# Spreading the five links of an expert pair over five positions, with u rows and v rows gathered apart

## What is computed

```python
def _peer(u, wq, keys, pu, pv):
    ...
    def block(args):
        xb, ib, gb = args
        act = jax.nn.gelu(jnp.einsum('thkd,td->thk', jnp.take(pu, ib, axis=0), xb), approximate=False) * gb
        return jnp.einsum('thk,thkd->td', act, jnp.take(pv, ib, axis=0))
```

## Time and profile before

| | us |
|---|---|
| median of 3 runs | 4927.02 (4921.54 to 4928.32) |
| the profiled execution | 4904.76 |
| its span, first instruction to last | 4903.0 |
| PE busy | 3672.0 (75%) |
| DVE busy | 3083.1 (63%) |
| POOL busy | 1563.8 (32%) |
| the gathers' packets, share of 16 DMA engines | 68.7% |

### The profile page before, as it was taken

How to read it: one execution, slowest core, us unless ns; L and a number is a source line. 1 busy time by engine, 2 the same in 40 slices (tenths; PEclk the granted TensorE clock), 3 DMA queues, 4 the chain that set the end, 5 groups by cost and what they waited for, 6 DMA issues and landing times.

```text
span 4903.0 us, 39211 instructions
## 1 busy us (share of the span) xinstructions
PE 3672.0 (75%) x11564; PEld 1854.1 (38%) x11564; DVE 3083.1 (63%) x7016; ACT 1117.4 (23%) x2809; POOL 1563.8 (32%) x1416
## 2 busy tenths in 40 slices
PE   8872987755887877976776589785488787797776
PEld 3430465531432432433443237563133343242222
DVE  1236537768686686684356654775867668668555
ACT  0101224411212212222421123441121221221111
POOL 0101223313344344343222312321333434444443
PEclk9985998867999999998988789887799999999999
DMA  8564785577999999999877868656699999999998
GB/s 295 180 239 178 281 293 215 207 272 290 404 384 421 379 402 420 375 394 368 327 287 299 349 231 322 219 202 258 260 406 383 411 398 391 421 373 415 391 421 357
DMA packets 314581, 1607.83 MB, mean 328 GB/s; under 512 B 41632, under 2 KB 82848, under 8 KB 144384
## 3 DMA queue, kind: packets, MB, share of 16 engines
q0 software_dynamic: 184320, 1342.26, 68.7%
q1 hardware_dynamic: 129952, 262.99, 14.8%
q10 hardware_dynamic: 96, 0.10, 0.0%
HBM read 1568.02 MB, written 37.20 MB: 327 GB/s over the span
## 4 chain that ended last, share of the span: by engine, by line
PE 37%; DMA 24%; DVE 21%; issue 7%; ACT 4%; SPq 4%; POOL 2%; POOLq 1%; DVEq 0%; ACTq 0%
DMA big<-in_experts,big 19%; PE bank L1979 15%; DVE big L1374 7%; PE bank L1729 4%; PE bank L1724 4%; PE bank L1955 3%; PE bank L1678 2%; POOL big L2088 2%; PE bank L1926 2%; DMA big<-in_w_in 1%; ACT big L1629 1%; DVE big L1282 1%; DVE big L1284 1%; DMA big<-in_iota 1%; SPq L862 1%
## 5 line engine op out<-in xcount | busy, mean ns | idle before, releaser
L1979 PE MATMUL bank<-big 128*128 128x512 f32 x4608 | 2333.6, 654 | 939.8 <-ACT big L1629 938.9
L2088 POOL DMA_INDIRECT big<-in_experts,big x1280 | 1452.2, 1135 | 3043.1 <-PE bank L1979 2593.1
L1374 DVE CUSTOM_DVE_ANT_0 big<-big 128x1024 f32<-128x1024 f32 x1280 | 1548.2, 1228 | 570.7 <-DMA big<-in_experts,big 569.9
L1979 PEld LDWEIGHTS bank<-big 128*128 128x128 f32 x4608 | 907.7, 206 | 2254.2 <-ACT big L1629 1267.8
L1629 ACT ACTIVATE big<-big 128x128 f32<-128x128 f32 x1152 | 407.8, 396 | 1201.7 <-DVE big L1352 1191.6
L1639 ACT ACTIVATE big<-big 128x2 f32<-128x2 f32 x640 | 130.9, 204 | 1600.8 <-DVE big L1374 1600.3
L1352 DVE TENSOR_TENSOR big<-big 128x2 f32<-128x2 f32 x640 | 108.5, 170 | 256.9 <-ACT big L1639 201.9
L1729 PE MATMUL bank<-big 128*128 128x256 f32 x960 | 220.7, 387 | 19.4 <-DMA big<-in_w_in 18.1
L1724 PE MATMUL bank<-big 128*128 128x128 f32 (+1 forms) x768 | 214.8, 435 | 2.0 <-DMA big<-in_w_in 2.0
L1729 PEld LDWEIGHTS bank<-big 128*128 128x128 f32 x960 | 185.0, 194 | 60.5 <-DMA big<-in_w_in 21.8
L1678 PE MATMUL bank<-big 128*2 128x512 f32 x384 | 172.5, 603 | 18.4 <-DMA big<-in_b_ada 11.0
(11 more groups left out here) (243 smaller groups left out, 2880.7 us busy)
## 6 DMA issues: line engine op xcount, KB each, us to landing
big<-in_w_ada SPq DMA_DIRECT2D x24, 2048.0 KB
big<-in_w_in SPq DMA_DIRECT2D x48, 1024.0 KB, 8.2
big<-in_experts,big POOLq DMA_INDIRECT x1280, 10.2
big<-modd SPq DMA_DIRECT2D x34, 512.0 KB, 21.8
big<-in_w_out SPq DMA_DIRECT2D x4, 4096.0 KB, 20.3
big<-in_peer_wq SPq DMA_DIRECT2D x4, 4096.0 KB, 39.1
y_d<-big SPq DMA_DIRECT2D x20, 512.0 KB, 5.6
big<-y_d SPq DMA_DIRECT2D x20, 512.0 KB, 11.0
```

Source lines behind the costliest of these rows:

```text
L1374: v_.tensor_tensor_reduce(ring[:, j, 0:D], ring[:, j, 0:D], EU[it % 2], 1.0, 0.0, ALU.mult, ALU.add, DOT[:, n % 16:n % 16 + 1]).then_inc(e ...
L1979: i = mm(ps[4 + h][:, :], DG[:, q % DIAGS * P:(q % DIAGS + 1) * P], ring[:, n % RING, D + 512 * h:D + 512 * h + 512], start=first, stop=last)
L2088: g_.indirect_dma_start(ring[:, n % RING, :], None, io["experts"], bass.IndirectOffsetOnAxis(ap=IDX[it % 2].bitcast(U32)[:, n:n + 1], axis ...
```

## The change

`apart(it)` is true for tiles 0, 4 and 5. In them the links of pair G stand at five positions: the dots at G, the GELU at G+1, `weigh` at G+2, `diag` at G+3, `v_pair` and DVE's own sums at G+4. In the other tiles all stays at G and G+1, but never ahead of an earlier pair, so the first pairs behind a heavy tile wait for its last ones. A v half is now needed four positions after its u half, and the ring still has eight slots. So in the heavy tiles, and for the first four pairs of the tile behind one (`halved`), u and v rows come by two gathers of 4 KB rows from two new inputs, `peer_u` and `peer_v` (the same numbers as `experts`). The u gather waits for the dot eight slots earlier (`e_dot`), the v gather stands one position behind its pair's dots and waits for the sum eight slots earlier. Consumers of v wait for a semaphore of their own (`e_gatv`). The tail of a heavy tile stands three positions later, and g0 of the tiles behind them goes from 7 to 10.

```diff
@@ order_of_work
-            (1, TICK["mx", 1, "smd"] + 1, TICK["mx", 2, "smd"], 7, 58),
+            (1, TICK["mx", 1, "smd"] + 1, TICK["mx", 2, "smd"], 10, 58),
...
+def apart(it):
+    return it in (0, 4, 5)
+
+def tail_place(it):
+    return 4 if apart(it) else 1
+
+def stands_at(near, far):
+    table, at = {}, 0
+    for G in range(DEPTH * TILES * PAIRS):
+        at = max(at, G + (far if apart(G // PAIRS) else near))
+        table.setdefault(at, []).append(G)
+    return table
+
+GELU_AT, WEIGH_AT, DIAG_AT, VALUE_AT = stands_at(0, 1), stands_at(1, 2), stands_at(1, 3), stands_at(1, 4)
+
+def halved(N):
+    G = N // 2
+    return apart(G // PAIRS) or (G >= 4 and apart((G - 4) // PAIRS))
+
+def value_loads(N):
+    return 16 * sum(1 for n in range(N % RING, N + 1, RING) if halved(n))
...
@@ DVE
+                        if halved(N):
+                            ve.wait_ge(e_gatv[n % RING], value_loads(N))
...
-                if G and (it < ALL or g == 0):
-                    weigh(G - 1)
+                for G in WEIGH_AT.get(at, ()):
+                    weigh(G)
+                for G in VALUE_AT.get(at, ()):
+                    value_sums(G)
...
-                if it and 2 <= g < 6:
-                    tail(it - 1, g - 1)
+                if it and 1 <= part < 5:
+                    tail(it - 1, part)
@@ ACT
-                if it < ALL or g == 0:
-                    diag(G - 1)
...
+                for G in DIAG_AT.get(it * PAIRS + g, ()):
+                    diag(G)
+                for G in GELU_AT.get(it * PAIRS + g, ()):
+                    gelu(G)
@@ PE
+                    if halved(N):
+                        pe.wait_ge(e_gatv[n % RING], value_loads(N))
...
-                if G and (it < ALL or g == 0):
-                    v_pair(G - 1)
+                for G in VALUE_AT.get(it * PAIRS + g, ()):
+                    v_pair(G)
@@ POOL
+                if halved(N):
+                    if N >= RING:
+                        ge.wait_ge(e_dot, N - RING + 1)
+                        ge.sem_inc(passed, 1)
+                    g_.indirect_dma_start(ring[:, n % RING, 0:D], None, io["peer_u"], offset(N)).then_inc(e_gat[n % RING], 16)
+                else:
+                    slot_done(N)
+                    g_.indirect_dma_start(ring[:, n % RING, :], None, io["experts"], offset(N)).then_inc(e_gat[n % RING], 16)
+
+            def gather_value(N):
+                j = N % RING
+                if N >= RING:
+                    slot_done(N)
+                g_.indirect_dma_start(ring[:, j, D:2 * D], None, io["peer_v"], offset(N)).then_inc(e_gatv[j], 16)
 
             def expert(it, g):
-                goal = min(2 * (it * PAIRS + g) + RING, ALL * SLOTS)
+                at = it * PAIRS + g
+                for N in (2 * at - 2, 2 * at - 1):
+                    if N >= 0 and halved(N):
+                        gather_value(N)
+                goal = min(2 * at + RING, ALL * SLOTS)
                 while len(issued) < goal and scored(len(issued) // SLOTS):
                     gather(len(issued))
```

More of the change, by code:

```diff
@@ L438, in build @@
         e_gat = [sem(f"e_gat{j}") for j in range(RING)]
+        e_gatv = [sem(f"e_gatv{j}") for j in range(RING)]
         e_vd = sem("e_vd")
@@ L882, in expert @@
             def expert(it, g):
-                if g == 3 and it in (1, 5, 6):
+                if it in (1, 5, 6) and g == tail_place(it - 1) + 2:
                     sp.wait_ge(e_tail.sem, e_tail.at(it - 1, "r02" if shared(it - 1) else "r01"))
@@ L886, in expert @@
                     load_g2(it)
-                if g == 6 and it:
+                if it and g == tail_place(it - 1) + 5:
                     sp.wait_ge(e_tail.sem, e_tail.at(it - 1, "xb"))
@@ L1352, in weigh, with value_sums @@
                 v_.tensor_tensor(AW[:, c], AG[:, c], GW[it % 2][:, 2 * g:2 * g + 2], ALU.mult).then_inc(e_aw, 1)
+            def value_sums(G):
+                it = G // PAIRS
                 for N in (2 * G, 2 * G + 1):
@@ L1364, in expert @@
             def expert(it, g):
-                G = it * PAIRS + g
-                if g == 1 and it:
+                at = it * PAIRS + g
+                part = g - tail_place(it - 1)
+                if it and part == 0:
                     tail(it - 1, 0)
-                if G and (it < ALL or g == 0):
-                    weigh(G - 1)
+                for G in WEIGH_AT.get(at, ()):
+                    weigh(G)
+                for G in VALUE_AT.get(at, ()):
+                    value_sums(G)
                 if it < ALL:
@@ L1630, in diag, with gelu @@
                                   scale=AW[:, N % 16:N % 16 + 1]).then_inc(e_dg, 1)
+            def gelu(G):
+                c = slice(2 * G % 16, 2 * G % 16 + 2)
+                ae.wait_ge(e_dot, 2 * G + 2)
+                a_.activation(AG[:, c], DOT[:, c], ACT.Gelu).then_inc(e_ge, 1)
             def expert(it, g):
-                G = it * PAIRS + g
-                if it < ALL or g == 0:
-                    diag(G - 1)
[L1636 to L1640, removed]
+                for G in DIAG_AT.get(it * PAIRS + g, ()):
+                    diag(G)
+                for G in GELU_AT.get(it * PAIRS + g, ()):
+                    gelu(G)
+                if it and g == tail_place(it - 1) + 3:
                     ae.wait_ge(e_tail.sem, e_tail.at(it - 1, "mv"))
@@ L2071, in _, with slot_done, offset @@
             issued, passed_tick = [], [-1]
+            def slot_done(N):
+                if summed_by_vector(N - RING):
+                    ge.wait_ge(e_vd, by_vector(N - RING))
+                else:
+                    ge.wait_ge(e_v, by_tensor(N - RING))
+                ge.sem_inc(passed, 1)
+            def offset(N):
+                it, n = divmod(N, SLOTS)
+                return bass.IndirectOffsetOnAxis(ap=IDX[it % 2].bitcast(U32)[:, n:n + 1], axis=0)
             def gather(N):
                 it, n = divmod(N, SLOTS)
[L2075 to L2081, removed]
+                if N == 0:
                     for u in range(3):
@@ L2096, in expert @@
                     issued.append(1)
-                assert it == ALL or len(issued) >= 2 * (it * PAIRS + g) + 2
+                assert it == ALL or len(issued) >= 2 * at + 2
             def scored(it):
```

15 lines of the change are left out of this document (7 added, 8 removed).

## The result

The changed kernel took 4868.92 us in the median of four runs (4866.19 to 4874.52), the kernel before 4924.28 beside it (4912.35 to 4928.32): a ratio of 0.9893, interval 0.9873 to 0.9913, 55 us less. The prediction said 4864, 63 us less.

A forecast was written before the change was run, and what follows sets the result against it. Light tiles were taken as DMA-bound, heavy tiles as engines waiting for each other. Terms -38 - 56 - 13 - 18 - 17 + 7 + 64 + 8 = -63 us took the 4927.0 median to 4864, range 4785 to 4930.

The forecast's parts named there:

- Rival (a): Scans of heavy tiles: all waits go, so they run at the busier engine, 71 us more gained, 4793; chance 0.15.
- (b): Hand-overs to light tiles cost their upper bound, 60 us more: 4924, no change; chance 0.14.
- (c): Heavy-tile stages: PE's and ACT's waits lie beside DVE's own work, stages give 0 instead of 87: +24, 4951; chance 0.13.
- (d): Gathers of half rows: a fixed 2.7 us each is paid in turn 400 times, +1080 us: 5944; chance 0.03.
- the barriers: Five barriers in heavy tiles: POOL's last gathers go out earlier, so drains end sooner, -38 us, bounds -15 and -54.
- Hand-overs: From tiles 0 and 5 to light tiles: POOL, DMA and PE work in turn for four pairs, +64 us, bounds +21 and +124.
- Scans: Heavy tiles' scans: position work fills engines' idle time, -56 us without barriers, bounds 0 and -127.
- Input projections: Beside tiles 4 and 5: part of PE's waits for diagonals goes, -13 us without barriers, bounds 0 and -24.
- Outputs: Heavy tiles' outputs: value sums ahead of the scoring matmuls on PE get done earlier, -18 us, bounds 0 and -35.
- Start of tile 5: Tile 4's tail stands three positions later, +16 us; three pairs fewer inside the stages give -9, net +7.
- Starts of tiles 0 and 4: First gathers carry only u halves, so less data stands ahead of first loads or dots: -17 us, bounds 0 and -20.
- More gathers: 400 slots come by two gathers, 496 us more on POOL, mostly in its waits: +8 us, bounds 0 and +40.

The follow-up runs named there:

- the first experiment: Changed kernel, with POOL issuing second halves of pairs 0 to 3 before whole rows of pairs 4 to 7 at both hand-overs: 4804.23 us, 0.9754.
- diagonals and sums together: Changed kernel's two gathers, but GELU with the dots, weigh one position behind, diagonals and value sums both one behind weigh: 4871.33 us, 0.9905 against the kernel before.
- sums alone: Changed kernel's two gathers, but GELU with the dots, weigh and diagonals one position behind, value sums one behind the diagonals: 4828.37 us, 0.9815 against the kernel before.

## Why the prediction was right, term by term

The sign, the range and the mechanism were right: 4869 against 4864, and the gain where it was looked for. That the total came so near is partly luck. The sum was made for the profiled execution, where it says -63 and the profiles say -39: hand-overs 17, outputs 10, input projections 6 and starts 3 us dearer than forecast, scans 8 us better. The medians differ by 55 us only because the profiled execution of before lay 20 us under its median and that of after 3.

Rival (a) did not come: 88 us of the scans went, barriers included, where it had 127 without them. (b) did not: tiles 1 and 6 took 393 us, under 400. (c) did not: the scans are not of the old length. (d) did not: 400 gathers by two, with no link moved, changed the time by 8 us, not by 1080. A stretch of tile 4 that is full with u and v halves (2225 to 2285 us) moves 387 GB/s, over the 380 named, and some 4% under the 403 of whole rows there before.

Of the profile's signs three came only in part. Tiles 1 and 6 grew by 45 and 44 us, not by some 30. PE's wait before the value sums fell by 156 us, as "some hundreds" loosely says: 323 less for diagonals, 119 more for v halves. The drains at barriers did not all end with the other engines. These are pieces of the chain of waits at two barriers of tile 4, behind its input projection and behind its scan, and the line of the drains.

```profile
2345.09 22.96 DMA big<-in_peer_u,big
...
2370.31 20.60 POOLq L377
...
2459.97 6.52 DMA mstate<-big
```
```profile
L377 POOLq DRAIN  x12: 34/12040/20592, 0.8 to 4491.1; - x12
```

By terms, with the barriers counted in the stages that they end, and the pair less in each stage of tile 5 (-9 in all) in that stage:

- **Hand-overs**, forecast +64, measured +81. The mechanism was right: links in turn on POOL, DMA and PE, which the first experiment took away. The first release came 45 us after position 60, not 36. The failed step is PE's "two slots of PE at 1.72 = 3.4": eight matmuls took 5.9 to 6.8 us in the chain above, at a granted clock of 0.66, a mean between the two levels, on a PE that waits 6 to 7 us for each landing. And ahead of the first release stand a sum of 3.8 us and the 5.5 us of ACT and DVE up to the tail, which the 36 left out. The price at the low clock stood in the earlier trace rows and was used for the upper bound only. That three links still took 44.7 us for the 41 forecast is luck: PE's 3 us too little and a landing of 5.7 to 7.4 us for 5.2 were set off by POOL, of whose 5.0 us a link only 1.2 lie on the path, since the other gathers go out while PE sums or the first half lands. And position 7 came 3 us behind the last link, not 7.
- **Scans**, with two barriers, forecast -80, measured -88. **Input projections**, with three, forecast -33, measured -27. Inside of both the barriers were taken for too much: -38 forecast, about -22 by the runs without a drain. The drains did not get shorter: at the barriers behind input projections and scans of tiles 0 and 5 they take 10.2 to 12.5 us (10.2 to 12.4 before), and in tile 4 they grew to over 20 us (9.7 and 7.5 before). The first of those ended last at its barrier; at the second the chain goes through a store of SP (`mstate` above), so there POOL's drain was not what the stage waited for. Four gathers in flight, for which the lower bound of -15 stood, do not explain the 20 us by themselves, since the list puts the same gathers ahead of the other barriers; the reason stays open. The scans' own -56 was too small: 88 less 3.9 for the pair less and at most 22 for barriers is at least 62 by these numbers. The step that was mis-sized is "a bit under half" of the 127 idle us, for which no row stood.
- **Outputs**, forecast -22, measured -12: nothing in tiles 0 and 5, 14 us in tile 4, the one with two slots on PE in each pair. There the runs left open what holds the other two; DVE's own work, as rival (c) had it for all stages, would fit.
- **Start of tile 5**, forecast +16, measured +15.
- **Starts of tiles 0 and 4**, forecast -17, measured -14. **More gathers**, forecast +8: the rest of the profile is +6. This term has not been measured by itself, since in the kernel with two gathers alone the order on POOL costs more than they do.

## What to carry to other kernels

A pipeline stretched over more positions paid at its ends here: where the stretched form meets the short one, look for a queue in which a transfer that the next step needs stands behind one that waits for that step, and put it ahead. Try the links one at a time: one position between diagonal and sum, with two gathers as well, gave some 90 to 100 us, all five positions 55, with 81 lost in the hand-overs (12 there). A drain at a barrier cost time here even in light tiles, which live on the queue that it stops.

## What was not expected of the hardware

POOL's drain with gathers out took 10.2 to 20.6 us at the barriers of the changed kernel; with none out, at the start, it took 34 ns (the line of the drains above).

The granted clock moved with the change too. The windows of tile 0's scan before, with two gathers alone, with diagonals and sums together, with sums alone, and with all five positions (above) hold the same 1152 matmuls:

```profile
722.30:982.90 260.60, 196.31 (x1152) 147.41 (x1152) 193.65 (x452) 106.89 (x273) 82.24 (x84) 0.80 0.58 207
```
```profile
722.60:1000.10 277.50, 208.95 (x1152) 158.46 (x1152) 192.78 (x452) 107.00 (x273) 124.27 (x120) 0.76 0.58 194
```
```profile
715.30:956.70 241.40, 187.55 (x1152) 141.76 (x1152) 186.40 (x452) 105.79 (x273) 142.22 (x121) 0.84 0.65 224
```
```profile
716.50:960.60 244.10, 194.40 (x1152) 154.09 (x1152) 185.36 (x452) 106.59 (x273) 143.50 (x122) 0.82 0.64 221
```

PE is busy 196 us before, 209 with two gathers alone and 188 with five positions, at granted clocks of 0.80, 0.76 and 0.86: means between the same two levels. PE's wait for diagonals alone does not decide it: with sums alone, where that wait is gone, PE is busy 194 us at 0.82, and with diagonals and sums together, where 28 us of it stay, 188 at 0.84. Of the 35 us that this scan gained, at most PE's 8 us less are of this kind; how much of them was on the path was not measured.

Of gathers in a row some take 0.94 us and some 1.9 to 2.0, as at 1149.70 in the timeline of the first experiment. The rule on the port that GpSimd shares with VectorE (the Trainium skill, "SBUF — State Buffer", section "SBUF: two separate sides") would allow such delays; no run here took VectorE's work away from them. In the trace of after the dots on VectorE (L1421) fill 54% of the time of the gathers above 1.6 us and 22% of that of those under 1.0 us, which fits but does not show the cause. It decided little: a gather's mean was 1.12 to 1.16 us with 400 gathers more, and 1.135 before.
